# Low rows moved to the place of the high ones within 512 bytes, two heads of attention values in turn, and a first inverse level made by transposes

## The reference

```
# delta layer, per head and chunk of tokens
lower = where(strict, (k*beta) @ k.T * decay, 0)
sol = triangular_solve(lower + eye, rhs)          # (I + L)^-1 rhs
# latent attention, per head
s = (q_nope @ k_nope.T + q_rope @ k_rope.T) * scale
out = softmax(s) @ v
# everywhere: h @ w, with h a normed and modulated row block
gu = h @ w_in
y = (silu(gu[..., :D_FF]) * gu[..., D_FF:]) @ w_out
```

## Time and profile before

| | |
|---|---|
| median of three runs | 2763.92 us (2762.91 to 2766.78) |
| profiled execution | 2759.97 us |
| its span | 2758.2 us |
| granted TensorE clock, mean | 0.967 |
| TensorE busy | 2552.7 us (93%) |
| TensorE weight loads busy | 2174.6 us (79%) |
| VectorE busy | 1860.6 us (67%) |
| ScalarE busy | 1092.0 us (40%) |
| GpSimd busy | 53.2 us (2%) |

### The profile page before, as it was taken

One profiled execution on the slowest core, in us unless ns is written; L12 is line 12 of the kernel. 1 busy time (PEld: TensorE's weight loads), 2 busy tenths in 40 slices (PEclk: granted clock), 3 DMA queues, 4 the chain that ended last, 5 costly groups with the idle time before them and its releaser, 6 DMA issues.

```text
span 2758.2 us, 37890 instructions
## 1 busy us (share of the span) xinstructions
PE 2552.7 (93%) x15170; PEld 2174.6 (79%) x15170; DVE 1860.6 (67%) x3164; ACT 1092.0 (40%) x1679; POOL 53.2 (2%) x56
## 2 busy tenths in 40 slices
PE   5889999786899899999997899999999999978998
PEld 4849999665799868888875588888888888866997
DVE  2648989544576767777845666677776565866666
ACT  4475448711354532222514452222342222534543
POOL 1000000021000000000000000000000000000000
PEclk8989999888999999999998999999999999999999
DMA  7877996422466536665322026555445454421663
GB/s 255 242 231 213 283 265 184 130 92 61 124 183 185 158 108 168 172 169 166 98 59 71 2 84 177 158 145 164 134 130 153 131 153 131 121 79 50 183 186 110
DMA packets 632564, 407.61 MB, mean 148 GB/s; under 512 B 27751, under 2 KB 588614, under 8 KB 631366
## 3 DMA queue, kind: packets, MB, share of 16 engines
q1 hardware_dynamic: 631712, 404.94, 51.6%
q10 hardware_dynamic: 678, 0.25, 0.0%
HBM read 404.09 MB, written 1.05 MB: 147 GB/s over the span
## 4 chain that ended last, share of the span: by engine, by line
PE 84%; DVE 8%; ACT 4%; DMA 2%; issue 1%; SPq 1%; ACTq 0%; POOL 0%; DVEq 0%
PE ps L1541 71%; PE ps L1563 2%; PE ps L1314 1%; PE ps L1578 1%; PE ps L1291 1%; PE ps L830 1%; PE ps L567 1%; DMA raw<-in_attn_w_in 1%; DVE w_lo L1879 1%; PE ps L838 1%; PE ps L840 1%; PE ps L1303 1%; DVE ada_acc L1896 0%; DVE tmp L2079 0%; DVE h_lo L2088 0%
## 5 line engine op out<-in xcount | busy, mean ns | idle before, releaser
L1721 ACT CAST w_hi<-raw 128x1024 fp32r<-128x1024 f32 (+3 forms) x557 | 554.4, 997 | 1227.6 <-PE ps L1541 1190.9
L1541 PE MATMUL ps<-h_hi,w_hi 128*128 128x258 f32 (+2 forms) x2952 | 974.0, 330 | 26.9 <-DVE h_lo L2088 13.7
L1541 PE MATMUL ps<-h_hi,w_lo 128*128 128x258 f32 (+2 forms) x2952 | 969.6, 328 | 0.0
L1541 PE MATMUL ps<-h_lo,w_hi 128*128 128x258 f32 (+2 forms) x2952 | 968.6, 328 | 0.0
L1879 DVE TENSOR_TENSOR w_lo<-raw,w_hi 128x1024 fp32r<-128x1024 f32 (+3 forms) x557 | 644.6, 1158 | 266.2 <-ACT w_hi L1721 263.2
L1541 PEld LDWEIGHTS ps<-h_hi,w_hi 128*128 128x128 f32 x2952 | 559.0, 189 | 88.7 <-issue 25.4
L1541 PEld LDWEIGHTS ps<-h_hi,w_lo 128*128 128x128 f32 x2952 | 559.8, 190 | 51.8
L1541 PEld LDWEIGHTS ps<-h_lo,w_hi 128*128 128x128 f32 x2952 | 560.5, 190 | 50.7
L1541 PE MATMUL ps<-a_hi,w_hi 128*128 128x256 f32 (+1 forms) x1056 | 354.6, 336 | 0.5 <-DVE a_lo L1934 0.5
L1541 PE MATMUL ps<-a_lo,w_hi 128*128 128x256 f32 (+1 forms) x1056 | 353.1, 334 | 0.0
L1541 PE MATMUL ps<-a_hi,w_lo 128*128 128x256 f32 (+1 forms) x1056 | 353.1, 334 | 0.0
(11 more groups left out here) (345 smaller groups left out, 2350.6 us busy)
## 6 DMA issues: line engine op xcount, KB each, us to landing
raw<-in_ffn_w_in SPq DMA_DIRECT2D x264, 512.0 KB, 4.7
ada_raw<-in_w_mod SPq DMA_DIRECT2D x120, 512.0 KB, 3.9
raw<-in_ffn_w_out SPq DMA_DIRECT2D x96, 512.0 KB, 5.2
ada_raw<-in_ada_w SPq DMA_DIRECT2D x40, 512.0 KB, 5.7
wide_rows<-in_ada_w SPq DMA_DIRECT2D x40, 512.0 KB, 5.0
raw<-in_ffn_w_out SPq DMA_DIRECT2D x48, 384.0 KB, 3.7
raw<-in_gdn_w_in SPq DMA_DIRECT2D x33, 512.0 KB, 4.1
raw<-in_w_in SPq DMA_DIRECT2D x26, 512.0 KB, 3.9
```

Source lines behind the costliest of these rows:

```text
L1541: last = mm(ps[0:m, slot, 0:n], w[:, slot, k * P:k * P + m], v[:, s0 + k, c0:c0 + n], start=(k == 0 and w is w_hi and v is hi), stop=(k == ...
L1721: nc.scalar.copy(w_hi[:, slot, 0:n], raw[:, slot, 0:n]).then_inc(s_hi, 1)
```

## The change

It has three parts.

1. 384 bytes (`apart`) are put between `h_hi` and `h_lo`. `h_lo` then stands at 128 bytes past a multiple of 512, as `h_hi` does. Tiles behind it shift by 384 bytes; `lat_hi` and `lat_lo` come to 192. The place of `a_hi` and `a_lo` is computed from that of `h_hi` and stays.
2. In the latent attention `pair_values` takes the values of two heads together, block by block in turn, in every second step. `pt2` gets a third buffer, and `stat2` moves to where `rot2` ends.
3. In the first level of the delta inverse `merge` transposes the mask. There is no copy to `inv_t`, no `merge2`, and the unit matrices are not copied: DVE writes unit minus transpose to `inv_x` and unit minus mask to `inv_y`. The second level's mask waits for `merged` in place of `merge_bx`, since the mask is read by that subtraction.

```diff
-        h_rows = [sb("h_hi", [P, KD * 2 * W], F32R), sb("h_lo", [P, KD * 2 * W], F32R)]
+        h_rows = [sb("h_hi", [P, KD * 2 * W], F32R)]
+        sb("apart", [P, 96])
+        h_rows.append(sb("h_lo", [P, KD * 2 * W], F32R))
...
-        pt2 = at("pt2", 36, [P, 2, 4, T])
-        stat2 = at("stat2", 44, [P, 16, 8])
+        pt2 = at("pt2", 36, [P, 3, 4, T])
+        stat2 = at("stat2", 26, [P, 16, 8])
...
                 for m in range(4):
-                    last = mm(ps[:, s, m * P:(m + 1) * P], inv_m[:, s, m], inv_x[:, s, m], start=True, stop=True)
+                    to = ps[:, s, m * P:(m + 1) * P]
+                    last = mm(to, inv_m[:, s, m], inv_x[:, s, m], start=True, stop=True) if level else tr(to, inv_m[:, s, m], ident)
...
                     for s in range(2):
-                        merge2(G, level, s)
+                        if level:
+                            merge2(G, level, s)
...
-                for level in range(7):
+                for level in range(1, 7):
...
-                V.tensor_copy(inv_x[:, s], spread(ident, 4))
-                V.tensor_copy(inv_y[:, s], spread(ident, 4))
...
             def merged(G, level, s):
-                n = (G * 7 + level) * 2 + s
+                if level == 0:
+                    dve.wait_ge(event("merge_bx"), G * 14 + s + 1)
+                    V.tensor_tensor(inv_x[:, s], spread(ident, 4), ps[:, s, :].rearrange("p (m n) -> p m n", m=4), ALU.subtract)
+                    V.tensor_tensor(inv_y[:, s], spread(ident, 4), inv_m[:, s], ALU.subtract).then_inc(event("merged"), 1)
+                    return
+                n = (G * 6 + level - 1) * 2 + s
...
                         if level:
-                            pool.wait_ge(event("merge_bx"), n - 1)
+                            pool.wait_ge(event("merge_bx" if level > 1 else "merged"), n - 1)
...
-            def values(i):
-                h, q0, k0, nk = units[i]
-                pe.wait_ge(event("mla_copied_act"), b0 + i + 1)
-                pe.wait_ge(event("mla_copied_dve"), b0 + i + 1)
-                if i % 2 == 0 and i >= 4:
-                    pe.wait_ge(s_h, st[2] + i // 2 - 1)
-                r = slice((i % 2) * DH, (i % 2 + 1) * DH)
+            def pair_values(b):
+                pe.wait_ge(event("mla_copied_act"), b0 + 2 * b + 2)
+                pe.wait_ge(event("mla_copied_dve"), b0 + 2 * b + 2)
+                if b >= 2:
+                    pe.wait_ge(s_h, st[2] + b - 1)
+                _, _, k0, nk = units[2 * b]
                 for k in range(nk // P):
-                    last = mm(ps[r, 6 + (i // 2) % 2, 0:T], v_tok2[:, k0 // P + k, h * DH:(h + 1) * DH], pt2[:, i % 2, k], start=(k == 0), stop=(k == nk // P - 1))
-                if i % 2:
-                    last.then_inc(event("mla_pair"), 1)
+                    for i in (2 * b, 2 * b + 1):
+                        h = units[i][0]
+                        r = slice((i % 2) * DH, (i % 2 + 1) * DH)
+                        last = mm(ps[r, 6 + b % 2, 0:T], v_tok2[:, k0 // P + k, h * DH:(h + 1) * DH], pt2[:, i % 3, k], start=(k == 0), stop=(k == nk // P - 1))
+                last.then_inc(event("mla_pair"), 1)
...
-                if i >= 2:
-                    values(i - 2)
+                if i >= 3 and i % 2:
+                    pair_values((i - 3) // 2)
```

More of the change, by code:

```diff
@@ L344, in build @@
         wide_rows = [nc.alloc_sbuf_tensor_at(name, [P, KD * 2 * W], F32, offset=int(h_at))
-                     for name, h_at in (("wide_rows_0", h_place), ("wide_rows_1", h_place + KD * 2 * W * 4))]
+                     for name, h_at in (("wide_rows_0", h_place), ("wide_rows_1", h_place + KD * 2 * W * 4 + 96 * 4))]
         coef = sb("coef", [P, 2, 4, KD])
@@ L944, in delta_scalar @@
                         act.wait_ge(event("merge_bx"), n + 1)
-                        if level == 0 and s == 0:
+                        if level == 1 and s == 0:
                             act.wait_ge(event("group_prepared"), 2 * G + 2)
@@ L1351, in mla_scalar @@
                     act.wait_ge(event("mla_turned"), b0 + i)
-                    nc.scalar.copy(pt2[:, (i - 1) % 2, 0:nk // P, 0:P], ps[:, 4, 0:nk].rearrange("p (k n) -> p k n", n=P)).then_inc(event("mla_copied_act"), 1)
+                    nc.scalar.copy(pt2[:, (i - 1) % 3, 0:nk // P, 0:P], ps[:, 4, 0:nk].rearrange("p (k n) -> p k n", n=P)).then_inc(event("mla_copied_act"), 1)
                 if i >= 3 and i % 2:
@@ L1395, in mla_vector @@
                     dve.wait_ge(event("mla_turned"), b0 + i)
-                    V.tensor_copy(pt2[:, (i - 1) % 2, 0:nk // P, P:T], ps[:, 5, 0:nk].rearrange("p (k n) -> p k n", n=P)).then_inc(event("mla_copied_dve"), 1)
+                    V.tensor_copy(pt2[:, (i - 1) % 3, 0:nk // P, P:T], ps[:, 5, 0:nk].rearrange("p (k n) -> p k n", n=P)).then_inc(event("mla_copied_dve"), 1)
                 if i >= 3 and i % 2:
```

## The result

| kernel | median of its runs, us | ratio to the kernel before, run beside it (95% interval) |
|---|---|---|
| changed | 2733.73 (2731.8 to 2734.6, 4 runs) | 0.989 [0.9873, 0.9907] |
| changed, once more | 2733.55 (2732.4 to 2734.0, 4 runs) | 0.988 [0.9863, 0.9896] |

The change is worth 30 to 33 us where 51 were forecast. The time lies in the range given and 20.7 us above the point. The profiled execution took 2734.58 us, 25.4 less than the profiled one of before. The difference to 30 is in the kernel before: the sum of the forecast was made against an execution at its fast end.

What follows compares the result with a forecast made beforehand. TensorE was taken as the bound (84% of the span, the weight product 71%). Terms of 17.8 + 11.3 + 11 + 11 = 51 us off the profiled 2759.97 gave 2709, stated as 2713 us for the median; range 2694 to 2742.

Steps and rivals of the forecast that it cites:

- 512 columns: Wide weight-product passes on `h`: with `h_lo` at the place of `h_hi`, 5 ns less over 3552 passes, 17.8 us.
- The twin of the same addresses: The 512-column passes that read `a`, at 226.7 ns, whose pace the wide passes on `h` were to take.
- Narrow passes: Weight-product passes of 258 and 256 columns: 2 ns less over 5664 passes, 11.3 us, between -5 and 28.
- Values in turn: Latent attention: two heads' interleaved values take one head's time, a 512-key pair 7.95 us; 11 us gained, between 5 and 14.
- First level by transposes: Delta inverse: transposes shorten the way to the second level and unit-matrix copies go; 11 us gained, bounds 6 and 13.
- 0.6 us of touch: Delta inverse, each group: GpSimd's first-half mask and DVE's second-half subtractions delay each other, between 0 and 1.1 us, taken as 0.6.
- the gain counted for the second group: Delta inverse, second group: first mask to second level's product falls from 9.19 to 5.1 us, gaining 4.1.
- (a): Rival: place is not the cause, or both rows in one place do not suffice; 2742 us, chance 0.08.
- (c): Rival: the two heads' values don't overlap and extra waits come on top; 2730 us, chance 0.06.
- (b): Rival: narrow passes gain 5 ns like the wide ones, 17 us more; 2696 us, chance 0.12.
- (d): Rival: narrow passes slow down, weight loads and row reads holding each other up; 2769 us at 8 ns, chance 0.03.
- (e): The case that all goes as forecast, between 2698 and 2730 us; chance 0.71.

Runs made afterwards that it cites:

- f1: Changed kernel with both halves of the normed rows `h` moved by 128 bytes, weights and `a` left in place; 2754.54 us in one run.
- e1: Kernel before with only the 384 bytes ahead of `h_lo` added; 2741.86 us, ratio 0.9915 to the kernel before.

## Why the forecast was right in sign and too high in size

- **512 columns, 17.8 us forecast.** Right: 232.0 to 226.8 ns, 3552 x 5.2 = 18.5 us. The twin of the same addresses was the right row to take, and f1 shows that the cause is the place of the rows.
- **Narrow passes, 11.3 us forecast.** Mis-sized: the step "so 2 ns are to be had if the narrow reads of h come to behave like those". They gained 0.5 ns, 5664 x 0.5 = 2.8 us. The row taken as the goal, `a` at 117.8 ns, owes its pace to something else (f1 has it at 113.8 in its old place). And the row taken as the start, 120.6, was one stage: the mean was 119.9. All of part 1 measured 23.5 us, from 18.5 to 28.5, for 29.1; the paces explain 21.3 of them.
- **Values in turn, 11 us forecast.** The mechanism and the pair's price were right (8.06 us for 7.95); a pair of 256 keys gave 0.6 us for 0.8. What failed is the allowance for the ends, "the first and last of each are bounded by filling and draining", which counted them at nothing. The drain costs more than before: TensorE has less to do in it, waits 2 us at a time, and the clock falls. Measured: 5.0 us alone (1.9 to 8.3), 1 to 4 in the changed kernel.
- **First level by transposes, 11 us forecast.** The 0.6 us of touch was right, and 5.10 us to the second level near the sum, though other work than the mask ended last there. The failed step is the gain counted for the second group, 4.1, which named no wait on the loads behind it. The last load of `wide_rows` is released by a product two levels ahead. From that product to the next it is 4.81 us in both kernels (707.52 to 712.33, 698.75 to 703.56), so it is asked for as early as before; it lands later, 7.7 us from that product's end for 5.5. That costs 2.2 us, and the low clock behind the wait 2.7. Why the load takes longer is open. Measured: 4.4 us (1.1 to 8.0).
- **The rivals.** (a), the place is not the cause, is out by e1 and f1. (c), the values don't overlap, is out by the sixteen passes in 1.95 us. (b) and (d) put 5 ns of gain and 8 of loss on the narrow passes, which moved by 0.5. The time 2733.7 lies above the 2698 to 2730 of the case (e): its mechanisms held in the main and its sizes didn't. It lies in the range given because that was widened for (a) and (c), which did not happen; that is luck.
- **The base.** The sum was set against a profiled execution 4 us under its median, and that median itself lay about 2 us under the later ones. The ratio is free of that: 0.988 to 0.989 for the 0.982 that 2713 / 2764 is.

## What to carry to other kernels

When work is taken from TensorE in a stage that ends in waits, look at the granted clock behind the stage before counting the gain: here filling the waits with idle products gave 6 to 8.5 us, more than part 2 itself, and filler behind a wait instead of inside it cost 3.7. Where a group of dependent steps gets shorter, list the loads that it waits for and what stands behind them: here one load and the low clock after it took back 4.9 us of the layer's gain. And a pace to be reached is only a forecast for a tile of the same width, blocks and place; the twin gave 18 of 18 us, the cousin 3 of 11.

## What the runs showed of the hardware

- The pace of a wide pass depends on where its rows stand within 512 bytes, with the weights at 128 throughout: 226.8 ns with the rows at 128 too, 232.5 with both halves at 256. The Trainium skill ("TensorE: Matmul & The Clock Gate", step 1 of Part 2) has two independent read ports and nothing taken from the running matmul; by that, as the prediction read it, the four rows of the table would be alike. They are not, and two kernels are 20.8 us apart by it; the measurement decides.
- Two fp32 products that fill output rows 0 to 63 and 64 to 127 in turn run at once: sixteen passes in 1.95 us, eight of one head alone in 1.94.
- The 256-column passes of `a` have two paces, 113.4 and 117.8 ns, at one address. They change from stage to stage and from kernel to kernel.
- The last load of 512 KB for `wide_rows`, with three weight loads of 512 KB issued right behind it, took 5.5 us from the end of the product that released it to its own product before the change (707.52 + 1.07 to 714.07), and 7.7 in the changed kernel (698.75 + 1.07 to 707.52). From issue to landing it took 5.0 to 5.2 us in the three traces without part 3 and 5.4 to 7.4 in the eleven with it. Why is open.
